# Key and removal key as one stationary operand in a chunked recurrence, and gate rows folded into the output weights

## The reference, cut to what matters

```python
def _headnorm(z, eps):
    mu = jnp.mean(zf, -1, keepdims=True)
    var = jnp.mean(jnp.square(zf - mu), -1, keepdims=True)
    return (zf - mu) * lax.rsqrt(var + eps)

def step(state, inp):                                  # _rwkv7_scan, 512 steps, 8 heads of 64
    removed = jnp.einsum('zhvk,zhk->zhv', state, kh_t)
    state = (state * w_t[:, :, None, :] - removed[..., None] * (kh_t * a_t)[:, :, None, :]
             + v_t[..., None] * k_t[:, :, None, :])
    return state, jnp.einsum('zhvk,zhk->zhv', state, r_t)

y = _headnorm(_dir_merge(y), GN_EPS) * gn_w + gn_b     # forward and backward runs added
out_r = (y + bonus).reshape(b, t, W_R) * g
...
x = _layernorm(ALPHA * x + g1 * (mixed[:, CTX_LEN:] @ w_out[l]), ln1_g[l], ln1_b[l])
ffn = _hier_moe(_modulate(x, sh2, sc2), ...)           # router, two of 32 experts for each token
x = _layernorm(ALPHA * x + g2 * ffn, ln2_g[l], ln2_b[l])
```

## Time and profile before

| | us |
|---|---|
| median of 3 runs (1979.87 to 1981.43) | 1980.43 |
| the profiled execution | 1981.74 |
| its span, first to last instruction | 1979.8 |
| PE busy | 1949.6 (98%) |
| DVE busy | 1125.0 (57%) |
| ACT busy | 469.2 (24%) |
| POOL busy | 249.7 (13%) |
| recurrence, 1248.3 to 1468.7 | 220.4 |
| tail, 1468.7 to 1538.2 | 69.5 |

### The profile page before, as it was taken

One profiled execution on the slowest core, in us unless ns is written; L12 is line 12 of the kernel. 1 busy time (PEld: TensorE's weight loads), 2 busy tenths in 40 slices (PEclk: granted clock), 3 DMA queues, 4 the chain that ended last, 5 costly groups with the idle time before them and its releaser, 6 DMA issues.

```text
span 1979.8 us, 35835 instructions
## 1 busy us (share of the span) xinstructions
PE 1949.6 (98%) x14899; PEld 1358.7 (69%) x14899; DVE 1125.0 (57%) x1894; ACT 469.2 (24%) x906; POOL 249.7 (13%) x239
## 2 busy tenths in 40 slices
PE   8999999999999999999999999999999999999997
PEld 6778979964778878995445565999985444444443
DVE  2697385654569657655668848545457333233324
ACT  3164110000426311000231145432333111110111
POOL 4684000000568100000000012000000000000000
PEclk9999999999999999999999999999998999999999
DMA  8333545544533355535821334200012999999995
GB/s 261 128 128 107 213 141 168 161 178 147 191 128 128 107 213 170 169 129 197 317 78 60 117 128 167 92 4 3 3 48 112 378 428 428 428 428 428 428 428 222
DMA packets 138891, 385.56 MB, mean 195 GB/s; under 512 B 16986, under 2 KB 64450, under 8 KB 127622
## 3 DMA queue, kind: packets, MB, share of 16 engines
q1 hardware_dynamic: 138757, 383.61, 51.6%
HBM read 382.55 MB, written 1.05 MB: 194 GB/s over the span
## 4 chain that ended last, share of the span: by engine, by line
PE 91%; DVE 7%; issue 1%; ACT 1%; DMA 0%; DVEq 0%; POOL 0%; ACTq 0%
PE psum L713 13%; PE psum L416 11%; PE psum L1754 10%; PE psum L3466 10%; PE psum L2629 8%; PE psum L3491 5%; PE psum L755 5%; PE psum L3396 3%; PE psum L438 3%; PE psum L609 3%; PE psum L3523 2%; PE psum L674 2%; PE psum L771 2%; PE psum L689 1%; PE psum L3042 1%; PE psum L2686 1%
## 5 line engine op out<-in xcount | busy, mean ns | idle before, releaser
L416 PE MATMUL psum<-arena,ring 128*128 128x256 f32 x1472 | 326.1, 380 | 0.0
L416 PEld LDWEIGHTS psum<-arena,ring 128*128 128x128 f32 x1472 | 276.0, 189 | 46.1 <-issue 7.2
L2629 PE MATMUL psum<-arena 64*64 64x64 f32 (+1 forms) x4320 | 179.7, 238 | 2.7 <-issue 1.5
L2629 PEld LDWEIGHTS psum<-arena 64*64 64x64 f32 x4320 | 171.4, 134 | 4.7 <-issue 2.7
L713 PE MATMUL psum<-arena,ring 128*128 128x128 f32 x1280 | 149.5, 275 | 0.0
L713 PEld LDWEIGHTS psum<-arena,ring 128*128 128x128 f32 x1280 | 146.1, 192 | 0.0
L1754 PE MATMUL psum<-arena,ring 128*128 128x512 f32 (+2 forms) x432 | 142.0, 490 | 0.0
L822 ACT ACTIVATE arena<-psum 128x512 f32<-128x512 f32 (+2 forms) x80 | 42.0, 544 | 348.5 <-PE psum L416 119.4
L1754 PEld LDWEIGHTS psum<-arena,ring 128*128 128x128 f32 (+1 forms) x432 | 81.1, 188 | 60.7 <-issue 55.4
L713 PE MATMUL psum<-arena 128*128 128x128 f32 x960 | 113.7, 274 | 0.0
L713 PEld LDWEIGHTS psum<-arena 128*128 128x128 f32 x960 | 110.4, 192 | 0.0
(11 more groups left out here) (517 smaller groups left out, 3104.6 us busy)
## 6 DMA issues: line engine op xcount, KB each, us to landing
ring<-in_w_in_dram SPq DMA_DIRECT2D x29, 2048.0 KB, 8.0
ring<-in_ffn_w_dram SPq DMA_DIRECT2D x46, 1024.0 KB, 7.8
arena<-in_ex_gate_dram SPq DMA_DIRECT2D x15, 2048.0 KB, 16.6
arena<-in_ex_up_dram SPq DMA_DIRECT2D x15, 2048.0 KB, 21.0
arena<-in_ex_down_dram SPq DMA_DIRECT2D x15, 2048.0 KB, 21.6
ring<-in_ex_gate_dram SPq DMA_DIRECT2D x14, 2048.0 KB, 13.9
ring<-in_ex_up_dram SPq DMA_DIRECT2D x14, 2048.0 KB, 18.3
ring<-in_ex_down_dram SPq DMA_DIRECT2D x14, 2048.0 KB, 20.4
```

The source lines that it names most:

```text
L416: ins = pe.matmul(bank[:, j, :], w[:, kc, c * P:(c + 1) * P], moving[:, kc, :], start=kc == 0, stop=kc == k - 1)
L2629: ins = pe.matmul(bank[r, u, :], a[r, u], b[r, u], start=i == 0, stop=i == len(terms) - 1)
```

## The change

It has three parts.

*Recurrence.* The removal keys and keys of a head lie side by side in `kb` (layout `u i` in place of `i u`), and `inner` takes them as one stationary operand of 128 columns. `mr` and `nr` go; two banks `kb` come, one for each head of a pair (`r`), with the key rows in one half of the bank's partitions and the removal key rows in the other (`K_ROWS`, `B_ROWS`). Stationary 64x128, moving 64x128. Each mask step on `mr` or `nr` in DVE, and each copy of an unmasked half in ACT, becomes two operations on 64 partitions. The order in the list is `kb 0, m, kb 1, gr`. `strict` and `pairs` count accordingly.

*Gate rows.* `gate_rows(0)` moves from the tail to the middle part, between `late_row(5)` and the last `head_vars`, with its diagonals and drains on ACT and its gate column on DVE. POOL, from the end of chunk 1 (`wu` of chunk 1 drained), adds the bias to the bonus, multiplies that by `g`, then `g` by the norm weight, and multiplies the output weights by the gate rows (16 operations of 128x512). DVE then adds the residue to the output product in one operation, without the product by the gate rows.

*Tail.* Four buffers for the deviations and four for the squares. PE takes the first quarter of tile 0's output products ahead of the variances, then the rest of tile 0 and half of tile 1's by columns of the inner dimension as DVE delivers them. The product by the reciprocal root comes after the one by `g`. The unread products ahead of tile 0 go, 3 remain ahead of tile 1, and 2 in place of 3 ahead of the totals. `layer_norm_2` begins with the operation that needs no deviation. ACT takes the first deviation of tile 1 ahead of the modulation of tile 0 and the second behind it; `gate_rows(1)` stands ahead of the router products of tile 0, and its drains on ACT behind the modulation of tile 0. At the last chunk ACT runs one root early, whose result nobody reads.

The diff, cut to its core (the helper functions of the head norm, shown above, go; the new loops take their place):

```diff
-    opened((("late_row", 4), 1), (("hv", 0), 2), (("hv", 1), 3), (("hv", 2), 5), (("late_col", 4), 1), (("hm", 3), 7), (("late_row", 5), 4))
+    opened((("late_row", 4), 1), (("hv", 0), 2), (("hv", 1), 3), (("hv", 2), 5), (("late_col", 4), 1), (("hm", 3), 7), (("late_row", 5), 4),
+           (("g1", 0), 3), (("g1", 1), 2))
...
-                keys += [("mr", c, z), ("m", c, z), ("nr", c, z)]
+                keys += [("kb", 0, c, z), ("m", c, z), ("kb", 1, c, z)]
...
+    keys += [("out2", tt, hf) for tt in range(TT) for hf in range(2)] + [None, None, ("g2", 0), ("g2", 1)]
...
+    gate_rows(pe, K, 0, K.diag_1)
...
+def gate_rows(pe, K, i, diag):
+    pe.wait_ge(K.sem["diag"], K.count("diag", 0, i + 1))
+    for hf in range(2):
+        key = (("g1", "g2")[i], hf)
+        pe.wait_ge(K.empty(key), K.empty_count(key))
+        for c in range(4):
+            ins = pe.matmul(K.bank(key)[:, c * P:(c + 1) * P], K.ones, diag[:, 4 * hf + c, :], start=True, stop=True)
+        ins.then_inc(K.full(key), 1)
...
+    act.wait_ge(K.full(("num", HP - 1)), K.full_count(("num", HP - 1)))
+    act.wait_ge(K.sem["hm_c"], K.count("hm_c", 0, HP - 1))
+    gate_diagonals(act, K, 0, K.diag_1)
...
+    for hf in range(2):
+        drain(("g1", hf), K.gate_1[:, hf, :])
...
+    dve.wait_ge(K.empty(("late_col", 1)), K.drained_count(("late_col", 1)))
+    gate_column(dve, K, link, 0)
...
-    return 2 * turn_of(c, z) if c < LAT else turn_of(c, z) + LAT * ZS
+    return 3 * turn_of(c, z)
...
-        each(("mr", c, z), 2, (t.b, kr))
+        for r in range(2):
+            pe.wait_ge(K.empty(("kb", r, c, z)), K.empty_count(("kb", r, c, z)))
+        for u in range(HP):
+            for r, rows in enumerate(HEAD_ROWS):
+                ins = pe.matmul(by_two(K.bank(("kb", r, c, z)))[:, u], t.kb[rows, u].rearrange("p i t -> p (i t)"), kr[rows, u], start=True, stop=True)
+                if u == HP - 1:
+                    ins.then_inc(K.full(("kb", r, c, z)), 1)
...
-        each(("nr", c, z), 2, (t.k, kr))
...
-            if c >= LAT:
-                drained(("mr", c, z))
...
-        if c >= LAT:
-            drained(("nr", c, z))
-        else:
-            pe.wait_ge(K.sem["pairs"], turn_of(c, z))
...
+        pe.wait_ge(K.sem["pairs"], turn_of(c, z))
...
-        drained(("wu", c, z), ("t1" if c >= LAT else "mr", c, z))
+        drained(("wu", c, z), *([("t1", c, z)] if c >= LAT else [("kb", r, c, z) for r in range(2)]))
...
-            drained(("wu", c, z), ("mr", c, z))
-        if c < LAT:
-            drained(("nr", c, z))
+            drained(("wu", c, z))
+        drained(*[("kb", r, c, z) for r in range(2)])
...
-                copy(("mr", c, z), t.own(c, BT), by_two(K.bank(("mr", c, z)))[:, :, 1, :])
+                for r, rows in enumerate(HEAD_ROWS):
+                    act.wait_ge(K.full(("kb", r, c, z)), K.full_count(("kb", r, c, z)))
+                    act.activation(t.own(c, BT)[rows], by_two(K.bank(("kb", r, c, z)))[B_ROWS, :, 1, :], ACT.Copy)
             act.wait_ge(K.sem["strict"], strict)
             copy(("m", c, z), t.own(c, KRT), by_two(K.bank(("m", c, z)))[:, :, 1, :])
+        if c == CHUNKS - 1:
+            act.activation(K.rt_l[:, 0, 4:5], K.ln_eps, ACT.Sqrt)
         for z in range(ZS):
             t = K.wkv[z]
...
                 act.wait_ge(K.sem["pairs"], turn_of(c, z))
-                copy(("nr", c, z), t.own(c, KT), by_two(K.bank(("nr", c, z)))[:, :, 1, :])
+                for r, rows in enumerate(HEAD_ROWS):
+                    copy(("kb", r, c, z), t.own(c, KT)[rows], by_two(K.bank(("kb", r, c, z)))[K_ROWS, :, 1, :])
...
-        tt_op(t.kb, K.k_and_a[:, :, :, at:at + CH], t.p_inv.unsqueeze(1).broadcast_to([P, 2, HP, CH]), ALU.mult).then_inc(K.sem["hats"], 1)
+        tt_op(t.kb.rearrange("p u i t -> p i u t"), K.k_and_a[:, :, :, at:at + CH], t.p_inv.unsqueeze(1).broadcast_to([P, 2, HP, CH]), ALU.mult).then_inc(K.sem["hats"], 1)
...
         n = 2 if lat else 1
-        key = ("mr", c, z)
-        dve.wait_ge(K.full(key), K.full_count(key))
-        ins = tt_op(t.strict_out(c, lat), by_two(K.bank(key))[:, :, 0:n, :], spread(K.masks[:, z, 0:n, :]), ALU.mult)
-        ins.then_inc(K.empty(key) if lat else K.sem["strict"], 1)
+        for r, rows in enumerate(HEAD_ROWS):
+            key = ("kb", r, c, z)
+            dve.wait_ge(K.full(key), K.full_count(key))
+            tt_op(t.strict_out(c, lat)[rows], by_two(K.bank(key))[B_ROWS, :, 0:n, :], spread(K.masks[B_ROWS, z, 0:n, :]), ALU.mult).then_inc(
+                K.sem["strict"], 1)
...
             K.sem["strict"], 1)
-        if lat:
-            dve.wait_ge(K.empty(key), K.drained_count(key))
-        else:
-            dve.wait_ge(K.sem["strict"], strict_of(c, z) - 1)
+        dve.wait_ge(K.sem["strict"], strict_of(c, z) - 1)
         tt_op(t.inv, t.powers(0)[:, :, 0, :], spread(K.one), ALU.add).then_inc(K.sem["inv_start"], 1)
...
-        key = ("nr", c, z)
-        dve.wait_ge(K.full(key), K.full_count(key))
-        ins = tt_op(t.pairs_out(c, lat), by_two(K.bank(key))[:, :, 0:n, :], spread(K.masks[:, z, 0:n, :]), ALU.mult)
-        ins.then_inc(K.empty(key) if lat else K.sem["pairs"], 1)
+        for r, rows in enumerate(HEAD_ROWS):
+            key = ("kb", r, c, z)
+            ins = tt_op(t.pairs_out(c, lat)[rows], by_two(K.bank(key))[K_ROWS, :, 0:n, :], spread(K.masks[K_ROWS, z, 0:n, :]), ALU.mult)
+            if lat:
+                ins.then_inc(K.empty(key), 1)
+                dve.wait_ge(K.empty(key), K.drained_count(key))
+        if lat:
+            dve.sem_inc(K.sem["pairs"], 1)
+        else:
+            ins.then_inc(K.sem["pairs"], 1)
...
         pool.wait_ge(link.sem, link.count())
+    pool.sem_inc(K.sem["wkv_tiles"], 1)
+    steady = ("wu", 1, ZS - 1)
+    pool.wait_ge(K.empty(steady), K.drained_count(steady))
...
+    pool.tensor_tensor(K.bonus, K.bonus, of_heads("r_norm_b"), ALU.add).then_inc(link.sem, 1)
...
+    pool.tensor_tensor(K.bonus, K.bonus, K.g_T, ALU.mult).then_inc(link.sem, 1)
...
+    pool.tensor_tensor(K.g_T, K.g_T, of_heads("r_norm_w"), ALU.mult).then_inc(link.sem, 1)
...
+    for hf in range(2):
+        pool.wait_ge(K.landed(("wo2", hf)), K.landed_count(("wo2", hf)))
+        pool.wait_ge(K.empty(("g1", hf)), K.drained_count(("g1", hf)))
+        w = K.weights(("wo2", hf), DC, BANK)
+        for kc in range(DC):
+            ins = pool.tensor_tensor(w[:, kc, :], w[:, kc, :], K.gate_1[:, hf, :], ALU.mult)
+        ins.then_inc(K.sem["wo_gated"], 1)
+        pool.wait_ge(K.sem["wo_gated"], K.count("wo_gated", 0, hf + 1))
     K.pool_base = link.base + link.n
...
-        unread_products(pe, K, ("h2T", 2 * tt), 4 - tt)
+        if tt == 1:
+            unread_products(pe, K, ("h2T", 2), 3)
...
+    for hp in range(HP):
+        norm_product("ym", "y_ready", hp, K.y_sum)
     for hf in range(2):
-        pe.wait_ge(K.landed(("wo2", hf)), K.landed_count(("wo2", hf)))
-    for tt in range(TT):
+        pe.wait_ge(K.sem["wo_gated"], K.count("wo_gated", 0, hf + 1))
+        pe.wait_ge(K.empty(("out2", 0, hf)), K.empty_count(("out2", 0, hf)))
+        out_product(0, hf, range(2))
+    for hp in range(HP):
+        norm_product("yv", "y_sq", hp, K.hn_sq)
+    for kc in range(2, DC):
         for hf in range(2):
-            pe.wait_ge(K.empty(("out2", tt, hf)), K.empty_count(("out2", tt, hf)))
-            out_product(tt, hf, range(DC // 2))
-    gate_rows(0)
-    for tt in range(TT):
-        for hf in range(2):
-            out_product(tt, hf, range(DC // 2, DC)).then_inc(K.full(("out2", tt, hf)), 1)
+            ins = out_product(0, hf, range(kc, kc + 1))
+            if kc == DC - 1:
+                ins.then_inc(K.full(("out2", 0, hf)), 1)
+        if DC // 2 <= kc < DC - 2:
+            for hf in range(2):
+                if kc == DC // 2:
+                    pe.wait_ge(K.empty(("out2", 1, hf)), K.empty_count(("out2", 1, hf)))
+                out_product(1, hf, range(kc - DC // 2, kc - DC // 2 + 1))
+    for hf in range(2):
+        out_product(1, hf, range(2, DC)).then_inc(K.full(("out2", 1, hf)), 1)
...
+        if tt == 0:
+            gate_rows(pe, K, 1, K.diag)
         router_products(tt)
-        if tt == 0:
-            gate_rows(1)
...
-    unread_products(pe, K, ("h2", 0, 0), 3)
+    unread_products(pe, K, ("h2", 0, 0), 2)
...
+    for hp in range(HP):
+        act.wait_ge(K.sem["y_c"], K.count("y_c", 0, hp + 1))
+        act.activation(K.hn_sq[:, hp, :], K.hn_c[:, hp, :], ACT.Square).then_inc(K.sem["y_sq"], 1)
+    for hp in range(HP):
+        key = ("yv", hp)
+        act.wait_ge(K.full(key), K.full_count(key))
+        act.activation(K.hn_v[:, hp, :], K.bank(key)[:, 0:T], ACT.Sqrt, bias=K.eps[:, 1:2]).then_inc(K.empty(key), 1)
+    gate_diagonals(act, K, 1, K.diag)
...
+    deviation("x3", 0)
+    deviation("x4", 0)
+    deviation("x3", 1)
+    modulated(0)
+    deviation("x4", 1)
...
+    modulated(1)
...
-    dve.wait_ge(K.sem[name + "_std"], K.count(name + "_std", 0, tt + 1))
```

(44 more changed lines are left out.)

127 lines of the change are left out of this document (37 added, 90 removed).

## The result

| kernel | median us | ratio to before (95% interval) |
|---|---|---|
| before, in the same comparison | 1981.34 (1979.61 to 1984.56) | |
| changed | 1987.25 (1983.61 to 1988.77) | 1.0026 (1.0017 to 1.0035) |

What follows compares the result with a forecast made beforehand. PE was taken as the bound, busy 98% of the span. Recurrence +4.35, middle +0.5, tail -7.5 and end -0.3 sum to -2.95 us, giving 1977.5 us from the median of the runs; range 1972 to 1982.

Steps and rivals of the forecast that it cites:

- the joined heads run together: Recurrence: a joined group takes 0.875 us plus 0.15 for shape; rival, heads in turn, 1.75, total 1991.5, chance 6%.
- shape changes cost: Recurrence: two tile shape changes per chunk pass at 0.15 us each; rival, they cost nothing, total 1973.8, chance 13%.
- The tail to `x4`: Tail: `x4` of token tile 0 at 29.4 us instead of 35.7, of tile 1 at 39.1 instead of 46.6.
- both cases of the tail: Tail: totals read at 52.0 us with the clock falling between router tiles, or 50.6 if it stays up, chance 18%.
- the recurrence's sum: Recurrence: per-chunk gains and waits over chunks 0 to 7 add to +4.35 us.
- Chunk 0: Recurrence, chunk 0: first level gains 1.2 us, but ACT's four half copies delay its first-power copy; net -0.4.
- The 0.48 for the unit operation: Recurrence, chunk 2: POOL lengthens DVE's unit operation, both inputs in SBUF, adding 0.48 us to PE's wait.
- the 1.6 for `hats`: Recurrence, chunk 2: each pair of `hats` operations some 1.1 us longer beside POOL; levels 5 and 6 lose 1.6.
- The rival "POOL shuts DVE out": Chunk 2: five DVE operations each wait 1.27 us instead of sharing, some 3.7 more, total 1981.2; chance 10%.
- The kept banks in chunks 3 to 7: Recurrence: PE waits for joined banks; +0.88 us in chunk 3, +0.59 in chunk 4, +0.45 each in 5 to 7.
- Chunk 1: Recurrence, chunk 1: no `gr` and a free bank for `st`; first level at 6.04 us against 7.1, -1.05.
- four unread products at 1.2 GHz (3.5): Tail, ahead of the totals: the second clock fall stays, so four unread records take 3.5 us; six took 5.23.

Runs made afterwards that it cites:

- banks_paced: Changed kernel with turned matrices and moved groups ahead of the joined banks in the list, and POOL's recurrence work split over chunks 2 to 4: 1968.0 us, ratio 0.9934.
- the second trace: A second profile of the changed kernel with nothing altered: one run, 1985.44 us, recurrence 230.6.
- the old list: The bank order the change itself gave the joined product, `kb 0, m, kb 1`; the changed kernel with it measured 1987.25 us, ratio 1.0026.
- tail_only: Changed kernel with the recurrence's products and bank list as before the change; gate rows, POOL's work and tail as changed: 1978.62 us, ratio 0.9978.
- tail_paced: Changed kernel with the recurrence's products and bank list as before the change, and POOL's work split over chunks 2 to 4: 1973.67 us, ratio 0.9958.
- paced: Changed kernel with POOL's recurrence work split over chunks 2, 3 and 4, each part behind its chunk's unit operation: 1982.21 us, ratio 0.9996.
- first_bank: Changed kernel with one pair swapped in the bank list, chunk 0's first pass, so the second joined bank precedes the turned matrix: 1984.42 us, ratio 1.0016.
- after_again: The changed kernel unaltered, profiled a second time: one run, 1985.44 us.

## Why the prediction was wrong, point by point

**Right.** In mechanism most of it: the joined heads run together (1.09 against 1.025), one DVE operation on 64 lanes costs like one on 128 (0.42 and 0.69), shape changes cost, the kept bank makes PE wait before `st` and `turned` from chunk 2 on, and chunk 2 is longer than chunk 3. The tail to `x4` came out to 0.1 us, and both cases of the tail occurred: 53.2 with the first fall of the clock (forecast 52.0), 49.9 without it in banks_paced (forecast 50.6).

**Wrong: the recurrence's sum.** This is the step that turned the sign: +4.35 forecast, +12.9 in the first trace, +10.2 in the second. Its waits were the right ones, but each was taken too short, and it put TensorE's clock at nothing. Worked out against the second trace, which has one fall of the clock in the recurrence where the first has three, 5.8 us are missing:
- *Chunk 0, 2.3.* Some 1.6 is the fall of the clock behind the middle part, which was in no term; it was there in all five traces of kernels with the joined product and the old list. The other 0.7 are the half operations: the first level did gain 1.2, but DVE's four key halves and ACT's copies of them, below, then hold PE longer than the step took (it stands still for 0.25 and 0.66).
- *Chunk 2, 1.5.* POOL: 2.1 forecast, 4.50 - 1.18 = 3.3 measured. The 0.48 for the unit operation did not come (it kept its 0.41), and the 1.6 for `hats` were 3.3: three of the four operations waited 1.07 to 1.10 us, most of the 1.27 of a POOL operation, where a shared 0.8 was assumed. In the earlier trace rows DVE's slow operation started 0.65 behind POOL's, so its delay of 0.81 can be what was left of that one, and no mixture. The rival "POOL shuts DVE out" had the mechanism, and with 5.8 for chunk 2 (2.1 + 3.7) too high a price. In the first trace two falls of the clock cost 3.1 more.
- *The kept banks in chunks 3 to 7, 1.5.* The mechanism was right; the term was mis-sized by 0.2 to 0.35 a chunk. The joined group costs 0.07 more than taken, and DVE's two half operations on 64x512 take 1.42, below, where two operations on 128x512 took 1.28.
- *Chunk 1, 0.5*: the same copies account for 0.3; the first level starts 6.34 behind the chunk's start instead of the forecast 6.04. The other 0.2 are not traced.

The chain of waits of the changed kernel in chunks 0 and 1, and its timeline of DVE in chunk 6:

```profile
1258.30 0.61 ACT arena L2777
...
1272.60 1.09 PE psum L2632 x16
...
1278.42 0.39 ACT arena L2777
...
1278.94 2.08 PE psum L2676 x64
```

```profile
1415.91 1.42 DVE L2842 TENSOR_TENSOR arena<-psum,arena 64x512 f32<-64x512 f32 x2 [2.67 <-PE psum L2632]
```

**Wrong: the tail**, -6.6 instead of -7.8, since the fall of the clock between the router tiles took in more than was forecast: it slowed half of tile 0's router products (1.92 instead of 1.08) and all six unread products (5.16 instead of 4.3). The path behind the router products was wrong too: the sum let four unread products at 1.2 GHz (3.5) end last, and it was DVE's routing. So the 1.2 us by which the totals missed are a difference of several errors.

**What the sum could have said.** It priced every wait as the time PE stands still, and asked of the clock only where the trace of before showed it low. A recurrence that gets a wait of 1.6 to 2.0 us in each of six chunks where it had none needs a rival in which the clock falls there, though the runs do not show that these waits bring the falls. With the one fall of the second trace at 1.6 us the forecast would have read -1.35 instead of -2.95, with the three of the first +1.85: the clock alone does not explain the miss.

## What to carry to other kernels

When a product saves time on the bottleneck, look at who holds its output bank and which group gets that bank next: here the same product was worth -7 or +7 us in the recurrence, by the order of one list (1.6 of the +7 is a fall of the clock). Work handed to an idle engine is free only if it does not share a resource with an engine on the path at that moment; the same 19 POOL operations cost 3 us in one piece, 4.6 with a fall of the clock behind them, and nothing when placed beside DVE operations that read PSUM (chunk 2 of tail_only and tail_paced). If one engine's order of groups changes, give the engine that reads them the same order.

## What the runs showed of the hardware

- A DVE operation with both inputs in SBUF beside POOL operations that read SBUF: 1.52 instead of 0.42 (256 elements per lane), 1.75 instead of 0.68 (512). At the chunk's start it was POOL that got longer: its third product took 2.04 where it takes 1.90 in the run paced, while DVE's unit operation, which had started 0.13 ahead of it, kept 0.41. The Trainium skill ("SBUF — State Buffer", "Who interferes with whom") says that such a pair excludes each other for a whole instruction and that the order of issue decides who waits. The trace agrees: three of the four `hats` operations waited 1.07 to 1.10, most of a POOL operation of 1.27, and the unit operation, which was there first, did not wait.
- A change of the stationary tiles from 64x64 to 64x128 cost 0.19 us, the change back 0.15. The Trainium skill ("TensorEngine Tiling (Array Packing)", "Tiling Modes") says that a change of tiling mode drains TensorE and that tiles of one mode run in parallel; the trace agrees with the second, 1.09 for two heads together where one after the other would be 1.75, and shows a price for the first, but not that it is a drain.
- TensorE's clock fell to 1.2 GHz behind a stretch in which PE was busy all the time, more than half of it with products of two moving columns (1246.89 to 1250.30 in first_bank), and did not fall behind waits of 1.45 and 1.96 us in one chunk (after_again). A fall cost 1.6 us in the recurrence.
